# Key products and masks of a delta-rule turn issued one turn earlier, the transposed inverse first, and the next stage's weights loaded in the odd turn

## What is computed

```python
x = x + 0.5 * swiglu(rmsnorm(x), f1_g, f1_u, f1_d)
h = rmsnorm(x)
sc_b, sc_c, sc_x, qkv_pre, a_raw, b_raw, z, gate_a, gate_b = split_columns(h @ w_in)
y_a = sc_b * causal_dwconv(sc_c * sc_x)                  # mixer A
y_b = gdn_mixer(qkv_pre, a_raw, b_raw, z, ...)           # mixer B, 8 heads of 128, below
x = x + (sig(gate_a) * (y_a @ w_a) + sig(gate_b) * (y_b @ w_b)) @ w_o
x = x + 0.5 * swiglu(rmsnorm(x), f2_g, f2_u, f2_d)

# mixer B, per chunk (its sequential core, chunked):
a_kk = beta * (k @ k.T) * dec_strict                     # the key products and their mask
u, w = solve(I + a_kk, [beta * v, beta * exp(g) * k])    # unit lower triangular
a_qk = (q @ k.T) * dec_incl
nu = u - w @ s
o  = (q * exp(g)) @ s + a_qk @ nu
s  = exp(g_last) * s + (k * exp(g_last - g)).T @ nu
y_b = rmsnorm(o, norm_g) * silu(z)                       # per head
```

## Time and profile before

| | us |
|---|---|
| median of 3 runs | 3372.26 (3371.04 to 3372.77) |
| the profiled execution | 3370.85 |
| its span, first to last instruction | 3369.1 |
| TensorE busy in the span | 3254.8 (97%) |
| VectorE, ScalarE, GpSimd busy | 1354.7, 913.1, 820.7 |
| mean granted TensorE clock | 0.983 |

### The profile page before, as it was taken

How to read it: one execution, slowest core, us unless ns; L and a number is a source line. 1 busy time by engine, 2 the same in 40 slices (tenths; PEclk the granted TensorE clock), 3 DMA queues, 4 the chain that set the end, 5 groups by cost and what they waited for, 6 DMA issues and landing times. The chain is left out here.

```text
span 3369.1 us, 50801 instructions
## 1 busy us (share of the span) xinstructions
PE 3254.8 (97%) x20030; PEld 3193.3 (95%) x20030; DVE 1354.7 (40%) x2258; ACT 913.1 (27%) x1379; POOL 820.7 (24%) x458
## 2 busy tenths in 40 slices
PE   8999999999999999999999999889999999999998
PEld 8999999998999999999999999779999999999997
DVE  4333333333677633433334343434314333333333
ACT  5111111112422333433444244311123111111113
POOL 2122111113222322323223232221242211111212
PEclk9999999999999999999999999889999999999999
DMA  4111111111323311212112121447212111111101
GB/s 135 44 37 50 44 44 44 44 31 41 105 87 99 105 46 56 78 51 69 58 51 76 51 84 41 143 145 266 71 46 63 50 44 44 44 44 37 45 24 54
DMA packets 275534, 226.44 MB, mean 67 GB/s; under 512 B 12171, under 2 KB 251915, under 8 KB 275441
## 3 DMA queue, kind: packets, MB, share of 16 engines
q1 hardware_dynamic: 275140, 225.08, 22.0%
q10 hardware_dynamic: 324, 0.41, 0.0%
HBM read 172.92 MB, written 52.54 MB: 67 GB/s over the span
## 5 line engine op out<-in xcount | busy, mean ns | idle before, releaser
L211 PE MATMUL ffn_bank<-ffn_h_hi,ffn_w_hi 128*128 128x368 f32 x2112 | 697.6, 330 | 6.9 <-DVE ffn_h_lo L620 6.9
L212 PE MATMUL ffn_bank<-ffn_h_lo,ffn_w_hi 128*128 128x368 f32 x2112 | 698.4, 331 | 0.0
L213 PE MATMUL ffn_bank<-ffn_h_hi,ffn_w_lo 128*128 128x368 f32 x2112 | 697.2, 330 | 0.0
L211 PE MATMUL mix_bank<-both_h_hi,mix_w_hi 128*128 128x368 f32 x1848 | 661.3, 358 | 5.1 <-DVE mix_pre L2014 3.2
L212 PE MATMUL mix_bank<-both_h_lo,mix_w_hi 128*128 128x368 f32 x1848 | 612.4, 331 | 0.0
L213 PE MATMUL mix_bank<-both_h_hi,mix_w_lo 128*128 128x368 f32 x1848 | 611.2, 331 | 0.0
L410 POOL TENSOR_TENSOR ffn_w_lo<-g_w_raw,ffn_w_hi 128x1024 fp32r<-128x1024 f32 x130 | 311.1, 2401 | 1189.8 <-ACT ffn_w_hi L406 1189.7
L819 POOL TENSOR_TENSOR mix_w_lo<-g_w_raw,mix_w_hi 128x1024 fp32r<-128x1024 f32 x77 | 193.4, 2512 | 891.5 <-ACT mix_w_hi L814 891.5
L211 PEld LDWEIGHTS ffn_bank<-ffn_h_hi,ffn_w_hi 128*128 128x128 f32 x2112 | 397.8, 188 | 8.1 <-issue 8.0
L213 PEld LDWEIGHTS ffn_bank<-ffn_h_hi,ffn_w_lo 128*128 128x128 f32 x2112 | 397.5, 188 | 0.0
L212 PEld LDWEIGHTS ffn_bank<-ffn_h_lo,ffn_w_hi 128*128 128x128 f32 x2112 | 397.3, 188 | 0.1
(11 more groups left out here) (287 smaller groups left out, 4151.7 us busy)
## 6 DMA issues: line engine op xcount, KB each, us to landing
g_w_raw<-in_w_in SPq DMA_DIRECT2D x73, 512.0 KB, 5.5
g_w_raw<-in_ffn_w_gate SPq DMA_DIRECT2D x44, 512.0 KB, 3.8
g_w_raw<-in_ffn_w_up SPq DMA_DIRECT2D x44, 512.0 KB, 3.9
g_w_raw<-in_ffn_w_down SPq DMA_DIRECT2D x44, 512.0 KB, 3.5
scratch_qkv<-mix_out SPq DMA_DIRECT2D x24, 552.0 KB, 2.8
turn_kq<-scratch_qkv SPq DMA_DIRECT2D x32, 256.0 KB, 3.5
scratch_x<-g_x SPq DMA_DIRECT2D x8, 552.0 KB, 6.9
scratch_z<-turn_z_out SPq DMA_DIRECT2D x8, 552.0 KB, 2.7
```

Of the source, the lines that this page charges most:

```text
L211: pe.matmul(out, w_hi, x_hi, start=first, stop=False)
L212: pe.matmul(out, w_hi, x_lo, start=False, stop=False)
L213: return pe.matmul(out, w_lo, x_hi, start=False, stop=last)
```

## The change

In every list the step `kk` is taken out of its turn and issued in the turn before, as `kk_next`: after `os` and one dense piece, ahead of the last dense piece, the last `evict` and `split`, and `out`. The seven dense pieces ahead of `E` become six. For the first turn `kk` is issued by hand: on PE after the last projection, on DVE ahead of the convolution of the last head's values, on POOL ahead of the last of three weight splits. In turn 15 `os` moves ahead of the last two dense pieces. In `zero`, DVE makes `w_inv` before `x_inv`. The loads of the merge stage's first two weight blocks move from the end of SP's program into step `nu` of the second odd turn.

```diff
--- before.py
+++ after.py
@@ -905,14 +905,12 @@
             piece[0] += 1
 
     order.append(("load", 0))
-    dense(3)
-    order.append(("kk", 0))
+    dense(2)
     order.append(("lu", 0))
     order.append(("q_sq", 0))
-    dense(1)
     order.append(("qk", 0))
     order.append(("vt", 0))
-    dense(1)
+    dense(2)
     order.append(("zero", 0))
     dense(2)
     for k in range(1, STAGES + 1):
@@ -948,13 +946,15 @@
     dense(2)
     order.append(("os", 0))
     dense(1)
+    order.append(("kk_next", 0))
+    dense(1)
     order.append(("out", 0))
     assert piece[0] == 36, piece
     return order
 
 
 TURN_ORDER = turn_order()
-NEXT_STEPS = ("load", "lu", "k_tok", "rate", "square", "dec", "eg", "sq", "sk", "mask", "scale")
+NEXT_STEPS = ("kk_next", "load", "lu", "k_tok", "rate", "square", "dec", "eg", "sq", "sk", "mask", "scale")
 WA = NQ + 3 * TURNS
 WA_UNITS = 4
 WA_PIECES = KC + 12 * (WA_UNITS - 1)
@@ -965,8 +965,8 @@
     order = []
     for name, k in TURN_ORDER:
         if name == "os":
-            order += [("dense", 35), ("evict", 8), ("ya_split", 0), ("os", 0), ("ya_split", 1)]
-        elif (name, k) in (("split", 2), ("dense", 35), ("evict", 8), ("rate", 0)):
+            order += [("os", 0), ("dense", 34), ("kk_next", 0), ("dense", 35), ("evict", 8), ("ya_split", 0), ("ya_split", 1)]
+        elif (name, k) in (("split", 2), ("dense", 34), ("dense", 35), ("kk_next", 0), ("evict", 8), ("rate", 0)):
             pass
         elif name == "k_tok":
             order.append(("square", 0))
@@ -1002,9 +1002,9 @@
     order.append(("load", 0))
     if g:
         dense(1)
-    order.append(("kk", 0))
-    order.append(("lu", 0))
-    if g:
+    if g == 0:
+        order.append(("lu", 0))
+    else:
         dense(1)
     order.append(("qk", 0))
     order.append(("kt", 0))
@@ -1241,7 +1243,7 @@
                 u = i * 2 + g
                 for name, k in TURN_ORDER:
                     if name in NEXT_STEPS:
-                        step(full[1 - g], name, k, u + 1, (u, full[g]), i + 1 if g else i, i, g)
+                        step(full[1 - g], "kk" if name == "kk_next" else name, k, u + 1, (u, full[g]), i + 1 if g else i, i, g)
                     else:
                         step(full[g], name, k, u, None, i, i, g)
 
@@ -1251,7 +1253,7 @@
             turn(NT - 1, 0)
             for name, k in last_full_order():
                 if name in NEXT_STEPS:
-                    odd_step(tails[0], name, k, TURNS, (TURNS - 1, full[1]))
+                    odd_step(tails[0], "kk" if name == "kk_next" else name, k, TURNS, (TURNS - 1, full[1]))
                 elif name in ("wa_split", "ya_split"):
                     odd_step(tails[0], name, k, TURNS, None)
                 else:
@@ -1260,7 +1262,7 @@
                 for name, k in odd_order(d.g):
                     if name in NEXT_STEPS:
                         if d.g == 0:
-                            odd_step(tails[1], name, k, TURNS + 1, (TURNS, d))
+                            odd_step(tails[1], "kk" if name == "kk_next" else name, k, TURNS + 1, (TURNS, d))
                     else:
                         odd_step(d, name, k, TURNS + d.g, None)
 
@@ -1387,6 +1389,9 @@
                         sp.wait_ge(ya_stored, 16 * (1 + KC))
                         sp.wait_ge(ya_lo, 3)
                         load_states(tails[0])
+                elif name == "nu" and d.g == 1:
+                    sp.wait_ge(w.lo_done, WA + WA_UNITS)
+                    slots.load_ahead(sp, ahead)
                 elif name == "ds":
                     sp.wait_ge(st_done, HG * d.g + k + 1)
                     sp.dma_start(sample_state[0][:, HG * d.g + k].rearrange("s k v -> k s v"), st[:, k, :, :]).then_inc(st_stored[k], 16)
@@ -1404,8 +1409,6 @@
                 sp.wait_ge(st_stored[k], 64)
             for k in range(2):
                 sp.wait_ge(wa_stored[k], 16 * (WA_UNITS // 2))
-            sp.wait_ge(w.lo_done, WA + WA_UNITS)
-            slots.load_ahead(sp, ahead)
 
         @block.gpsimd
         def _(pool):
@@ -1478,8 +1481,9 @@
             shared(full[0], "lu", 0, 0, None, 0)
             w.split_lo(pool, H - 1, 3, 4)
             shared(full[0], "mask", 0, 0, None, 0)
-            for j in range(1, 3):
-                w.split_lo(pool, H - 1, 3, 4 + j)
+            w.split_lo(pool, H - 1, 3, 5)
+            shared(full[0], "kk", 0, 0, None, 0)
+            w.split_lo(pool, H - 1, 3, 6)
             turns(pool, step, odd_step)
 
         @block.tensor
@@ -1716,7 +1720,7 @@
                         pe.matmul(U.ps(unit)[:, 0:3 * P], d.kdec[:, k, :], flat(nu_seg[:, 3 * r:3 * r + 3, :]),
                                   start=True, stop=True).then_inc(U.done, 1)
 
-            sums_at = {(4, 2): "k_tok", (5, 0): "dec", (5, 1): "eg"}
+            sums_at = {(4, 2): "k_tok", (5, 0): "dec", (5, 1): "eg", (6, 2): "kk"}
             for n in range(4, 7):
                 w.wait(pe, H - 2, 3, n)
                 for b in range(NB):
@@ -1974,9 +1978,9 @@
                 elif name == "zero":
                     dve.wait_ge(d.on.bk_ready, d.masks(h) + 1)
                     eye = over_heads(ident[0:n, 0:n], d)
-                    dve.tensor_tensor(d.x_inv[:, :, :], eye, d.bk[:, 0, :, :], ALU.subtract).then_inc(d.on.x_started, 1)
                     U.wait_done(dve, u, "T0")
                     dve.tensor_tensor(d.w_inv[:, :, :], eye, d.ps("T0", n, n), ALU.subtract).then_inc(U.sem("T0"), 1)
+                    dve.tensor_tensor(d.x_inv[:, :, :], eye, d.bk[:, 0, :, :], ALU.subtract).then_inc(d.on.x_started, 1)
                 elif name in ("Za", "Zb"):
                     U.wait_done(dve, u, f"{name}{k}")
                     dve.tensor_tensor(d.z, d.x_inv[:, :, :], d.ps(f"{name}{k}", n, n), ALU.subtract).then_inc(U.sem(f"{name}{k}"), 1)
@@ -2021,6 +2025,8 @@
                     if scale_first and j == 0:
                         dve.wait_ge(prep_act, 4)
                         shared(full[0], "k_tok", 0, 0, None, 0)
+                    if scale_first and j == 2:
+                        shared(full[0], "kk", 0, 0, None, 0)
                     dve.wait_ge(silu_done, i * 3 + (j + 1))
                     W = GL - GP
                     ch.link(dve, dve.tensor_scalar(conv[:, j, 0:W], row[:, 0:W], gc_w[:, j, 0:1], None, ALU.mult))
```

## The result

The changed kernel takes 3389.36 us (median of 5 runs, 3384.96 to 3390.99) against 3372.26 before: a ratio of 1.0047 with a 95% interval of 1.0036 to 1.0059, so it is slower by 0.47%, some 17 us. The forecast was 3370.0, no change. The profiled execution took 3389.36 us too (span 3387.6), 18.5 more than that of before.

What follows compares the result with a forecast made beforehand. TensorE was taken as the bound, its longest wait T0's for POOL's mask. Boundaries 0.7, first turn -1.4, last full turn 1.0 and merge stage 2.0 gave 2.3 us off 3372.3: 3370.0, range 3362.5 to 3376.5.

Steps and rivals of the forecast that it cites:

- a case with 0.09: Slower rival: split waits at `vt` and `E` make PE's clock fall at turn boundaries; 3378 to 3388 us, chance 0.09.
- T0's wait: Transpose in `zero` waits for POOL's mask, 27.1 us in 17 of 18 turns; claimed to go in the full turns.
- the bank of `vt`: Turn boundary: `vt` needs the PSUM bank ACT's logarithm reads; forecast waits at `vt` about 0.3 and 1.4 us.
- the moment: Turn boundary: when ACT or DVE answers the turn's last dense piece; `out` starts 5.11 (even) or 6.08 us (odd) later.
- The lock: Even boundaries: POOL's `lu`, issued first, blocks DVE's two-SBUF-input `out`; `E` 0.23 us later than before, in 8 turns.
- That is all that a boundary can give: Turn boundaries: with `E` bound by `w_inv`, at most 0.37 us (even) or 0.36 us (odd) gained, whatever T0's wait.
- the other edits of order: Shifted evictions and splits, and masks ahead of the weight split delaying SP's next weight load: costed at nothing.
- the first turn: Masks slow DVE's value convolution, wait moves to `E`, PE restarts at low clock: 1.4 us lost.
- The odd turns: Last full turn into odd turns: waits move from `os` and T0 to `kt` and `Y1`; gain 1.0, from -1 to 4.
- The third: Slower rival: PE's clock falls at 7 to 15 boundaries, about 1.2 us each; 3378 to 3388 us, chance 0.09.
- The first: Rival: `lu` does not block `out` and the first turn's convolution isn't held up; 9.0 us gained, 3363.3, chance 0.18.
- The second: Rival: all of T0's wait is won, with `E` free; 33 us gained, 3339 us, chance 0.06.

Runs made afterwards that it cites:

- two experiments that cure it in different ways: Changed kernel with the next even turn's loads issued ahead of SP's wait for `out`: 3372.28 us; changed kernel with `k_tok` behind two dense pieces: 3360.42 us.
- the fastest kernel: Changed kernel with `k_tok` behind two dense pieces, loads ahead of `out`, `zero` ahead of `qk`, `vt` behind two dense pieces, `lu` behind `qk`: 3339.91 us.
- the run with the old order put back: Changed kernel with `k_tok` behind two dense pieces, and `os` and `kk` of the last full turn where they were before: 3361.47 us.

## Why the prediction was wrong, point by point

The time was 19 us above the forecast and outside its range, and the sign is that of a case with 0.09.

**Right.** T0's wait went and gave almost nothing, because `w_inv` and the bank of `vt` stood right behind it: `vt` waits 0.35 and 1.32 us (forecast 0.3 and 1.4), `E` starts 1297.14 - 1287.93 = 9.21 us after the moment in odd ends (forecast 9.17) and 8.56 in even ones. The lock was there, `lu` holding `out` up by 0.32 us (I had let `out` end 0.6 us behind `lu`, 6.45 us after the moment; it ended 0.55 behind, at 6.18, since `lu` was over at 5.63 and not at 5.85). `E` waits 0.24 us in even ends (forecast 0.6), which lost 0.13 each, with 0.23 forecast. In the merge stage the first large matmul comes 2289.00 - 2275.58 = 13.4 us after the last `os` in place of 2269.76 - 2254.11 = 15.7, so 2.2 us sooner with 2.0 forecast; the loads alone, in the kernel before, won 1.1 us, not clear of none.

**The step that failed** is the sentence "That is all that a boundary can give". I followed the boundary up to `E` and took what stands behind `E` as moving with it. `k_tok` doesn't: it hangs on a load that SP issues behind `out`, and I had just written that `out` stays where it is. Under "the other edits of order" I looked at SP's queue for the weight load and not for the three input loads in front of it. The trace of before had it in its list of DMA issues (between 1280 and 1296 us; count, size of one, median us from issue to landing):

```profile
turn_kq<-scratch_qkv SPq DMA_DIRECT2D x2, 256.0 KB, 4.0
```

SP issued the two within 1.39 us from 1287.65, so by this median the second landed between about 1292 and 1293 (it was 1292.47), and `k_tok` followed at 1292.62, right behind `ks`. A row without a wait says that the limit is not later, not how much earlier it is. The term was 7 x -0.36 = -2.5 us and is +13.0; two experiments that cure it in different ways take 14 us off, and a third, which takes one cure out of the fastest kernel, puts 8.8 us back.

**A size that failed** is the first turn, +1.4 forecast and +6.3 measured, as worked out under the table. Its parts were named: the convolution above 7 us (8.07), the wait moved to `E`, `E` hardly later (14.82 us after the last projection's last eviction at 1156.33, before 1169.82 - 1155.30 = 14.52). But with `E` where it was, one dense piece less is done by then, and I left these 0.84 us out. And I priced the half clock at 1.4 us from a single stop. Here `k_tok`, the same load again, stopped PE a second time 5 us after the first, and PEclk was 0.52, 0.50 and 0.70 over 12 us. Without that second stop, in the run with `k_tok` moved, `os` of the first turn comes 2.9 us sooner, counted from the weight split (1220.47 - 177.30 in place of 1223.06 - 177.01), though `E` waits 6.17 us there too. The experiment that put the mask back took 5.3 us off the first turn.

**The odd turns** lost 1.1 us, 0.3 with the same work, with a gain of 0.8 forecast in the same stretch. The waits came where the forecast had them (`kt` 4.71, `Y1` 2.58 us). With 4.4 us between two kernels that have the same program there, neither sign is shown, nor does the run with the old order put back tell (1.05 us, within the spread).

**The rivals.** The third had the sign and nearly the time (3378 to 3388) but another cause: in the full turns the clock stayed at 1.00 from 1230 to 2110 us, through all waits of 1.7 to 2.0 us; it fell in the first turn, and in one boundary of one experiment at a wait of 1.95. The first, against which I had put that POOL's durations hardly vary (the earlier trace rows have `lu` from 1.18 to 2.59 us), didn't come: the lock was there. The second, all of T0's wait won and 3339 us, was put at 0.06 because of two limits; with these two and the loads out of the way the kernel takes 3339.91. That this meets the 3339 is luck: 12.5 of the 32.9 us are what moving `k_tok` gives in the kernel before. Against that kernel with `k_tok` moved, the fourteen turns are 16.0 us shorter (836.0 and 820.0 us), of the 7 x (0.74 + 1.70) = 17.1 us that T0 waited in them.

## What to carry to other kernels

When work is moved ahead of a point, everything behind that point comes nearer to whatever is tied to the point and does not move: follow the engine past the first step that is late, up to the next load or semaphore of every queue, and work out its slack even where the trace shows no wait. A step that waits for nothing may be there with 0.1 us to spare. And a wait that is removed is worth what the second limit leaves; here three more (`w_inv`, the bank of `vt`, the loads) had to be moved as well before T0's 17 us of waiting in fourteen turns became 16 us of time.

## What the runs showed of the hardware that was not expected

The place of one short transpose decided how often ACT changes its function table: 14 loads of 1.28 us fewer, and some 10 us of the kernel's time, with no cost seen elsewhere. The TensorE clock at its two levels (1.2 and 2.4 GHz) made 4.4 us of difference in a stretch of 130 us between two kernels with the same instructions in it. Waits of 1.7 to 2.0 us left the clock at 1.00 in the seven boundaries of the changed kernel, and one of 1.95 was followed by a fall in another; what decides is open.
